# Expert gather, expert sum and out projection in the short float format; sum and norm tile by tile, recurrence roots ahead of the gates

## Chip, cores and metric

The kernel runs on 1 core of one Trainium2 chip. The metric is the device time of one execution in microseconds (us), the median of several runs; lower is better.

## What is computed

The reference runs two transformer blocks on 512 tokens of width 1024, all in float32. What matters here is the end of the first block and the mixing part of the second:

```python
# first block, end: hierarchical mixture of experts, 4 groups x 8 experts, top 2 in the best group
w_top, e_idx = lax.top_k(p_exp, TOP_K)                      # two experts for each token
w_top = w_top / jnp.sum(w_top, -1, keepdims=True) * p_group
for e in range(N_EXPERTS):                                  # 32 experts, 1024 -> 256 -> 1024
    hid = jax.nn.silu(t @ w_gate[e]) * (t @ w_up[e])
    out = out + combine[:, e:e + 1] * (hid @ w_down[e])
x = x + gate2[:, None, :] * ffn
# second block
f = swiglu(rms_norm_2(h, ffn1_norm_pre), w_gate, w_up, w_down)     # "ffn1", width 2816
h = h + 0.5 * rms_norm_2(f, ffn1_norm_post)
# mixing: dilated attention, and a linear recurrence  h_t = a_t h_(t-1) + b_t
b = jnp.sqrt(-jnp.expm1(2.0 * log_a)) * (gate_x * xc)
gates = jax.nn.sigmoid(gl)
merged = gates[:, :, 0] * attn_d + gates[:, :, 1] * rec_d
h = h + rms_norm_2(merged @ w_out, mix_norm_post)
f = swiglu(...)                                                    # "ffn2", then the last residual
```

## The kernel before

One program, written engine by engine: PE, ACT, DVE, POOL and SP each have a fixed list of instructions (bottom of the file), and they meet at counting semaphores (`nxt(engine, name)` waits for the next count). Activations lie transposed (features on partitions) in `hT`; the residual `X` lies by tokens, four tiles of 128.

**Two kinds of matmul.** A matmul on plain float32 operands leaves two records in the trace. In the ffn stages and most of the mixing the operands are split into a high part, rounded to the short format (`F32R`), and the rest: `three` (L2128) multiplies high*high, high*low and low*high, and each of these leaves one record. ACT makes the high part of each 1 MB weight slot (`act_high`, L2110), POOL the low part (L2115 and L2457, one subtraction of 128x2048), SP loads the next slot when `slots_used` says that PE has read the slot three places before (L2444).

**Router and gather (L1580 to L1756).** PE makes the logits (L1585) and turns the normed tokens back (`pe_h2`), ACT copies them to `h2tok` (`act_h2`, L1634) and only then computes the two exponentials of the router (`act_route`). DVE chooses the experts (L1663 to L1710); PE ranks the tokens (L1596 to L1602, L1598 counts tokens before, L1601 counts all); DVE gives each of the two choices of a token a place among 1024 (`r_place`, L1726). It then compares a row of numbers with the places, twice for each of 4 tiles (L1735), POOL adds each pair to the selection matrix `m_G` (L1756), and DVE makes the weighted matrix `m_C` (L1740, L1742). PE starts the gather (L1611, 64 float32 matmuls of 512 columns) when all four tiles of `m_G` are there, then turns `m_C` (L1619). `dve_more_list` lists the experts with more than 128 tokens; here there is one such item, which runs ahead of the others (`pe_more`).

**Experts (`pe_moe`).** Each of 32 experts reads 128 gathered places: gate and up (L1814), Silu on ACT, product on DVE (L1885), down (L1822), copied by ACT and DVE into `m_yT`.

**Sum (L2006 to L2044).** PE turns `m_yT` back to rows (L2015), ACT and DVE copy them, and PE sums with the weights of `m_CT` (L2023, 64 float32 matmuls). DVE adds the result times `gate2` to `X`. All engines meet, then `act_norm1`/`dve_norm1` norm the tiles, PE turns them (`pe_xT`, L2200), ACT and DVE split them (L2286, L2335), and ffn1 starts.

**Recurrence (L2954 to L2985).** For each of 8 blocks m DVE does a reciprocal (L2964), waits for the root from ACT (`act_roots`, L2924), does L2967, L2968, L2970, the scan (L2972) and, for m below 3, two attention products (L2951). On ACT `act_roots` stands between the first and the second slot of the gate `gl1`. At the end DVE multiplies by the Gelu (L2981), ACT takes the high parts (L2665), with `mix_high(REC_W + 2)` (the high part of a weight slot) behind the first of them, and DVE the low parts (L2984); then PE multiplies by `rec` (8 halves) and DVE merges each half (L2752 frees the bank, L2754 adds).

**Out projection (`pe_out2`, L2987).** 64 float32 matmuls of 512 columns on `merged` and raw weight slots; the last two slots are done tile by tile, and `act_between`/`dve_between` norm each tile as it comes.

## Time and profile before

| | us |
|---|---|
| median of 3 runs | 2647.72 (2644.58 to 2651.13) |
| the profiled execution | 2647.43 |
| its span, first to last instruction | 2645.6 |
| PE busy | 2415.2 (91%) |
| DVE, ACT, POOL busy | 863.8, 613.6, 597.4 |
| DMA | 277.97 MB, 105 GB/s in the mean |

The stages, by the profile's times from the start of the span: first block's attention and recurrence to 594, its out projection to 651, router and gather 667 to 795, experts 799 to 1164, sum and norm 1165 to 1249, ffn1 1249 to 1640, mixing 1645 to 2261, ffn2 2261 to the end. PE's busy time is modelled at each matmul's end, so the pace of matmuls is read from the distance of their starts.

### The profile page before, as it was taken

Reading aid. Unit: us, or ns where it says so; the run is one execution under the profiler, and the core shown is the slowest. Engines: PE = TensorE matmul, PEld = TensorE weight load, DVE = VectorE, ACT = ScalarE, POOL = GpSimd, SP = SyncE. Lnnn points to the kernel's source line nnn. Section 1 sums busy time; section 2 is a strip of 40 time slices with the busy share of each in tenths; the row PEclk is TensorE's granted clock in tenths of the full one; section 3 lists DMA queues with packets and bytes.
Section 4 is the critical chain, followed back from the end, with each engine's and each line's share of the span. In section 5 each row is a group of like instructions: output and inputs, shape, how many; then the busy total and the mean of one; then the engine's idle time right before and its main releaser. Section 6 shows DMA issues by size and latency. Waiting matters only on the chain.

```text
span 2645.6 us, 30301 instructions
## 1 busy us (share of the span) xinstructions
PE 2415.2 (91%) x12189; PEld 1873.7 (71%) x12190; DVE 863.8 (33%) x1288; ACT 613.6 (23%) x940; POOL 597.4 (23%) x216
## 2 busy tenths in 40 slices
PE   6998789958498999997999997999999979899998
PEld 5644468853448999984888786888875854688786
DVE  4275544431441111112222204143452952322302
ACT  2023223320201000012222214143323311322212
POOL 0023023300100000010344342333422420344432
PEclk7998879989599999998999998999999989899999
DMA  8221400001114888840322223212332221333222
GB/s 278 64 80 60 163 32 1 1 1 48 58 41 139 296 295 295 296 161 0 93 89 90 94 96 97 96 64 92 107 113 81 89 87 55 96 95 95 96 80 88
DMA packets 220357, 277.97 MB, mean 105 GB/s; under 512 B 9703, under 2 KB 199107, under 8 KB 220260
## 3 DMA queue, kind: packets, MB, share of 16 engines
q1 hardware_dynamic: 211744, 267.49, 30.6%
q10 hardware_dynamic: 7140, 4.87, 0.7%
q0 software_dynamic: 1376, 4.26, 0.5%
q8 instruction: 68, 1.11, 0.2%
q14 instruction: 29, 0.24, 0.0%
HBM read 272.36 MB, written 4.24 MB: 105 GB/s over the span
## 4 chain that ended last, share of the span: by engine, by line
PE 82%; DVE 8%; ACT 3%; issue 2%; DVEq 2%; ACTq 1%; DMA 1%; POOL 1%; POOLq 0%
PE bank L2131 39%; PE bank L1814 9%; PE bank L1822 4%; PE bank L618 3%; PE bank L1611 2%; PE bank L586 2%; PE bank L1504 2%; PE bank L2023 2%; PE bank L1294 1%; PE bank L434 1%; PE bank L2994 1%; DVE arena L2967 1%; PE bank L1287 1%; PE bank L2880 1%; PE bank L2899 1%
## 5 line engine op out<-in xcount | busy, mean ns | idle before, releaser
L2131 PE MATMUL bank<-hT_high_split,ring_split 128*128 128x512 f32 x2496 | 797.2, 399 | 8.1 <-DVEq L2232 5.6
L2131 PEld LDWEIGHTS bank<-hT_high_split,ring_split 128*128 128x128 f32 x2496 | 471.4, 189 | 120.0 <-DVEq L2232 6.3
L2115 POOL TENSOR_TENSOR ring_split<-ring,ring_split 128x2048 fp32r<-128x2048 f32 x66 | 304.4, 4614 | 1014.4 <-ACT ring_split L2110 1014.4
L2131 PE MATMUL bank<-hT_split,ring_split 128*128 128x512 f32 x1248 | 492.0, 394 | 0.0
L2110 ACT ACTIVATE ring_split<-ring 128x2048 fp32r<-128x2048 f32 x104 | 199.1, 1916 | 669.7 <-DMA ring<-in_ffn_w_up 197.4
L2131 PEld LDWEIGHTS bank<-hT_split,ring_split 128*128 128x128 f32 x1248 | 235.8, 189 | 57.2 <-issue 0.2
L2457 POOL TENSOR_TENSOR ring_split<-ring,ring_split 128x2048 fp32r<-128x2048 f32 x38 | 175.8, 4627 | 350.7 <-ACT ring_split L2110 350.7
L1814 PE MATMUL bank<-arena,ring 128*128 x2048 | 235.8, 276 | 5.5 <-issue 5.5
L1814 PEld LDWEIGHTS bank<-arena,ring 128*128 128x128 f32 x2048 | 233.1, 193 | 5.7 <-issue 5.7
L2131 PE MATMUL bank<-ring_split,hid_high_split 128*128 128x512 f32 x704 | 224.7, 401 | 8.1 <-DVE hid_low_split L2242 7.2
L2131 PEld LDWEIGHTS bank<-ring_split,hid_high_split 128*128 128x128 f32 x704 | 133.8, 191 | 42.2 <-DVE hid_low_split L2242 8.0
L2237 DVE TENSOR_TENSOR arena<-arena,bank 128x512 f32<-128x512 f32 x44 | 30.2, 687 | 348.4 <-ACT arena L2213 345.0
L2131 PE MATMUL bank<-ring_split,hid_low_split 128*128 128x512 f32 x352 | 140.8, 400 | 0.0
L1822 PE MATMUL bank<-arena,ring 128*128 128x128 f32 x1024 | 119.4, 275 | 0.0
L1822 PEld LDWEIGHTS bank<-arena,ring 128*128 128x128 f32 x1024 | 116.8, 192 | 0.0
L1885 DVE TENSOR_TENSOR arena<-arena,bank 128x256 f32<-128x256 f32 x32 | 13.5, 421 | 226.5 <-ACT arena L1864 226.5
L2240 DVE CAST hid_high_split<-arena 128x512 f32 (+1 forms) x44 | 80.7, 1833 | 7.0 <-issue 6.4
L618 PE MATMUL bank<-hT,ring 128*128 128x512 f32 x192 | 82.6, 592 | 0.0
L1350 POOL TENSOR_TENSOR arena<-arena,constants 128x512 f32<-128x512 f32 x40 | 50.8, 1286 | 128.5 <-PE bank L1287 79.6
L2131 PEld LDWEIGHTS bank<-ring_split,hid_low_split 128*128 128x128 f32 x352 | 67.0, 190 | 16.4
L1611 PE MATMUL bank<-arena 128*128 128x512 f32 x128 | 57.9, 616 | 22.3 <-POOL arena L1756 22.3
L2342 DVE TENSOR_SCALAR arena<-arena 128x1024 f32<-128x1024 f32 x2 | 5.3, 2652 | 202.5 <-DMA constants<-in_mix_norm_pre 102.0
(421 smaller groups left out, 2770.0 us busy)
## 6 DMA issues: line engine op xcount, KB each, us to landing
ring<-in_w_in SPq DMA_DIRECT2D x45, 1024.0 KB, 5.1
ring<-in_w_gate SPq DMA_DIRECT2D x32, 1024.0 KB, 5.5
ring<-in_w_up SPq DMA_DIRECT2D x32, 1024.0 KB, 8.0
ring<-in_w_down SPq DMA_DIRECT2D x32, 1024.0 KB, 7.5
ring<-in_ffn_w_gate SPq DMA_DIRECT2D x22, 1024.0 KB, 5.3
ring<-in_ffn_w_up SPq DMA_DIRECT2D x22, 1024.0 KB, 5.4
ring<-in_ffn_w_down SPq DMA_DIRECT2D x22, 1024.0 KB, 4.9
ring<-in_w_ada SPq DMA_DIRECT2D x16, 1024.0 KB, 5.2
```

Of the source, the lines that this page charges most:

```text
L586: mm = pe.matmul(banks[t][:, :], lhs(4 * half + k, t), w[:, k, :], start=(half == 0 and k == 0), stop=(half == 1 and k == 3))
L618: mm = pe.matmul(bank[j][:, :], w[:, k, j * P:(j + 1) * P], hT[:, k, :], start=(k == 0), stop=(k == KD - 1))
L1504: mm = pe.matmul(bank[2 * t + half][:, :], lhs(k, t), w[:, kk_, 512 * half:512 * half + 512], start=(k == 0), stop=(k == 2 * n_slots_ - 1))
L1611: mm = pe.matmul(bank[n % 8][:, :], h2tok[:, t, k * P:(k + 1) * P], m_G[:, t, 512 * half:512 * half + 512], start=(t == 0), stop=(t == NT ...
L1814: mm = pe.matmul(dst[:, c:c + CAP], w[:, u, k, f * P:(f + 1) * P], m_xT[:, k, bass.ds(at, CAP)], start=(k == 0), stop=(k == KD - 1))
L1822: mm = pe.matmul(dst[k // 4][:, (k % 4) * CAP:(k % 4 + 1) * CAP], w[:, f, k * P:(k + 1) * P], hid[:, f, :], start=(f == 0), stop=(f == 1))
L2023: mm = pe.matmul(bank[2 * t + half][:, :], m_CT[:, s, t * P:(t + 1) * P], m_y[:, s, 512 * half:512 * half + 512], start=(s == 0), stop=(s ...
L2110: act.activation(high(n), raw(n), ACT.Copy).then_inc(S(f"{tag}_high"), 1)
L2115: pool.tensor_tensor(low(n), raw(n), high(n).bitcast(F32), ALU.subtract)\
L2131: mm = pe.matmul(dst, left[l], right[r], start=start and n == 0, stop=stop and n == 2)
L2240: dve.tensor_copy(at[0], hid)
L2457: pool.tensor_tensor(low(n), raw(n), high(n).bitcast(F32), ALU.subtract).then_inc(S("mix_low"), 1)
```

## The change

- *Gather.* `m_G` is made on DVE alone (a comparison with a row of 1024 numbers, `iota_wide`, for the first choice, and a second one that adds), without POOL's addition, and a tile of it can be used as soon as it is there. It holds zeros and ones in the short format. The tokens are split into `h2_high` (ACT, beside `h2tok`) and `h2_low` (POOL, four subtractions of 128x1024), so the gather is two products of 64 short matmuls each. ACT does the group exponential ahead of the copies and the second one between them.
- *Ranks.* Five matmuls instead of fourteen.
- *Weights.* `m_C` is gone. PE makes `w_row` (the weight of each place, on all partitions) in 32 short matmuls, and DVE multiplies each expert's hidden values by it, one more 128x256 product for each expert. PE turns `m_G` instead of `m_C`.
- *Sum.* The turned rows are split into `y_high` (ACT) and `y_low` (DVE); the sum is 128 short matmuls, first the left half of the columns, then the right half tile by tile. Each tile goes into the norm at once; the meeting of the engines is gone. The high part of ffn1's second slot is made after the norm.
- *Recurrence.* `act_roots` stands ahead of the first slot of `gl1`.
- *Out projection.* The four weight slots of `w_out2` and `merged` are split, and `three` is used: 192 short matmuls.

```diff
@@ pe_route
-            nxt(pe, "h2_ready", NT)
+            nxt(pe, "h2_ready")
+            nxt(pe, "r_M")
+            pe.matmul(bank[2][:, 0:P], con("before"), r_M.rearrange("p t e -> p (t e)"), start=True, stop=False)
+            for t in range(NT - 1):
+                pe.matmul(bank[2][:, 32 * (t + 1):P], ones,
+                          r_M[:, t, :].unsqueeze(1).broadcast_to([P, NT - 1 - t, N_EXP]), start=False, stop=(t == NT - 2))
+            mm = pe.matmul(bank[2][:, P:2 * P], ones, r_M.rearrange("p t e -> p (t e)"), start=True, stop=True)
+            mm.then_inc(S("r_ranks"), 1)
+            nxt(pe, "h2_ready", NT - 1)
             pe.drain().then_inc(S("o_free"), 1)
...
+            for t in range(NT):
+                nxt(pe, "r_G")
+                for n in range(8):
+                    gather(n, h2_high, t, t == 0, False)
+            nxt(pe, "h2_low", NT)
+            for n in range(8):
+                for t in range(NT):
+                    mm = gather(n, h2_low, t, False, t == NT - 1)
+                mm.then_inc(S("m_x_ps"), 1)
+            for n in range(8, 2 * KD):
+                nxt(pe, ("m_x_even", "m_x_odd")[n % 2])
+                for part in (h2_high, h2_low):
...
+            nxt(pe, "w_split")
+            for half in range(2):
+                nxt(pe, ("m_x_even", "m_x_odd")[half])
+                terms = [(t, c, w) for t in range(NT) for c in range(2) for w in (r_wh, r_wl)]
...
@@ act_route
             act.drain().then_inc(S("r_gexp"), 1)
+            act_h2(act, 1)
+            act_h2(act, 2)
             nxt(act, "r_diff")
             act.activation(r_w2, r_m2, ACT.Exp).then_inc(S("r_wexp"), 1)
+            act_h2(act, 3)
+            act_h2(act, 0)
@@ dve_route
+            nxt(dve, "iota_wide")
+            for t in range(NT):
+                dve.tensor_scalar(m_G1[:, t, :], iota_wide, r_place[:, 0, t:t + 1], None, ALU.is_equal)
                 dve.drain()
+                dve.scalar_tensor_tensor(m_G[:, t, :], iota_wide, r_place[:, 1, t:t + 1], m_G1[:, t, :].bitcast(F32),
+                                         ALU.is_equal, ALU.add).then_inc(S("r_G"), 1)
@@ pool_route
+            for t in (1, 2, 3, 0):
+                nxt(pool, "h2_ready")
+                i = pool.tensor_tensor(h2_low[:, t, :], h2tok[:, t, :], h2_high[:, t, :].bitcast(F32), ALU.subtract)
+                i.then_inc(S("h2_low"), 1)
@@ dve_moe, hidden
+                dve.drain()
+                dve.tensor_tensor(m_hid[:, b], m_hid[:, b], weights_at(at), ALU.mult)
@@ pe_moe_end
             for s in range(8):
+                turn(0, s)
             nxt(pe, "gate_taken")
+            for s in range(8):
+                if s < 4:
+                    turn(1, s)
+                for t in range(NT):
+                    mm = add(bank[4 + t][:, :], 0, s, t)
+                if s >= 4:
+                    turn(1, s)
+            mm.then_inc(S("m_sum_ps"), 1)
+            nxt(pe, "y_low", 4)
+            for t in range(NT):
+                for s in range(8):
+                    mm = add(bank[t][:, :], 1, s, t)
                 mm.then_inc(S("m_sum_ps"), 1)
+                if t >= 2:
+                    pe_xT(pe, t - 2, FIRST_BANKS)
@@ dve_moe_end
+            nxt(dve, "m_sum_ps")
+            for t in range(NT):
+                total(t, 0)
+            nxt(dve, "post_loaded", 16)
             for t in range(NT):
                 nxt(dve, "m_sum_ps")
+                total(t, 1).then_inc(S("x_new"), 1)
+                if t:
+                    dve_unit(dve, t - 1)
+                if t >= 2:
+                    dve_xT(dve, t - 2, FIRST_BANKS)
@@ act_mix
+            act_roots(act)
             for n in range(GL1, YR):
-                if n == GL1 + 1:
-                    act_roots(act)
                 mix_high(act, n + 2)
...
+            for n in range(4):
+                if n < 3:
+                    mix_high(act, OUT2 + n)
+                nxt(act, "m_merged")
+                for m in (2 * n, 2 * n + 1):
+                    i = act.activation(merged_hi[m], merged[:, m, :], ACT.Copy)
+                i.then_inc(S("m_high"), 1)
+            mix_high(act, OUT2 + 3)
@@ dve_mix
                 dve.drain().then_inc(S("m_merged"), 1)
+                if n > REC_W:
+                    dve_merged(dve, n - REC_W - 1)
+            dve_merged(dve, 3)
+        def dve_merged(dve, n):
+            nxt(dve, "m_high")
+            for m in (2 * n, 2 * n + 1):
+                i = dve.tensor_tensor(merged_lo[:, m, :], merged[:, m, :], merged_hi[m].bitcast(F32), ALU.subtract)
+            i.then_inc(S("m_low"), 1)
@@ pe_out2, add
+                return three(pe, bank[2 * t + half][:, :], (merged_hi[k][:, c], merged_lo[:, k, c]),
+                             [x[:, kk_, r] for x in w], k == 0, k == KD - 1)
```

## Rows read from the trace of the kernel before

**Rows 1.** The page, part 4: the chain that ended last, by engine.
```profile
PE 82%; DVE 8%; ACT 3%; issue 2%; DVEq 2%; ACTq 1%; DMA 1%; POOL 1%; POOLq 0%
```
**Rows 2.** Windows: stretch, busy (x count) of PE, PEld, DVE, ACT, POOL, clock, DMA.
```profile
704.00:712.00 8.00, 6.05 (x28) 5.92 (x28) 1.54 (x8) 0.00 (x0) 0.00 (x0) 0.50 0.00 0
712.00:732.00 20.00, 0.00 (x0) 0.00 (x0) 19.16 (x18) 0.00 (x0) 10.12 (x4) 0.50 0.00 0
732.00:738.00 6.00, 5.68 (x7) 2.48 (x8) 5.74 (x6) 0.00 (x0) 0.26 (x1) 0.52 0.01 3
819.00:1164.00 345.00, 344.94 (x3071) 344.94 (x3072) 34.92 (x63) 30.87 (x63) 0.00 (x0) 0.99 0.81 274
1229.00:1250.00 21.00, 7.45 (x34) 6.35 (x35) 12.61 (x19) 13.33 (x23) 0.00 (x0) 0.67 0.00 0
2050.00:2126.00 76.00, 75.78 (x324) 60.37 (x322) 73.57 (x42) 26.59 (x29) 31.92 (x7) 1.00 0.28 91
```
**Rows 3.** The chain of waits in order of time: start, length, what.
```profile
732.32 57.91 PE bank L1611 x128
1173.31 55.19 PE bank L2023 x128
1249.26 237.26 PE bank L2131 x1008
2191.43 34.59 PE bank L2994 x80
```
**Rows 4.** Timeline, router and gather: start, length, engine, line, what.
```profile
701.09 0.22 ACT L1639 ACTIVATE arena<-arena 128x16 f32<-128x16 f32 x1
712.44 0.17 DVE L1729 TENSOR_SCALAR arena<-arena 128x8 f32<-128x8 f32 x1
725.26 2.34 POOL L1756 TENSOR_TENSOR arena<-arena 128x1024 f32<-128x1024 f32 x1 [2.33 <-DVEq L1737]
734.10 0.75 DVE L1740 TENSOR_SCALAR arena<-arena 128x1024 f32<-128x1024 f32 x1
734.94 1.28 DVE L1742 SCALAR_TENSOR_TENSOR arena<-arena 128x1024 f32<-128x1024 f32 x1
791.05 3.69 PE L1619 MATMUL bank<-constants,arena 128*128 128x128 f32 x32 [0.83 <-issue]
799.50 7.41 PE L1814 MATMUL bank<-arena,hT 128*128 x64 [0.37 <-issue]
```
**Rows 5.** Groups of DVE instructions by line and form: busy, mean ns.
```profile
L1735 DVE TENSOR_TENSOR arena<-constants,arena 128x1024 f32<-128x1024 f32 x8 | 15.9, 2033 | 0.4
L2697 DVE TENSOR_SCALAR arena<-arena 128x2 f32<-128x2 f32 x8 | 10.1, 1265 | 0.6
```
**Rows 6.** Timeline, end of the experts.
```profile
1165.30 7.18 PE L2015 MATMUL bank<-constants,arena 128*128 128x128 f32 x64 [1.01 <-DVEq L1893]
1166.40 0.69 DVE L2035 COPY arena<-bank 128x512 f32<-128x512 f32 x1 [1.27 <-PE bank L2015]
1233.72 0.29 ACT L2281 ACTIVATE rstd<-ss,constants 128x1 f32<-128x1 f32 x1
```
**Rows 7.** Timeline, recurrence.
```profile
2049.75 0.69 DVE L2967 SCALAR_TENSOR_TENSOR arena<-arena 128x512 f32<-128x512 f32 x1 [24.93 <-ACT arena L2924]
2088.09 4.65 POOL L2457 TENSOR_TENSOR ring_split<-ring,ring_split 128x2048 fp32r<-128x2048 f32 x1 [6.48 <-ACT ring_split L2110]
2088.37 4.91 DVE L2967 SCALAR_TENSOR_TENSOR arena<-arena 128x512 f32<-128x512 f32 x1
2133.03 4.83 POOL L2457 TENSOR_TENSOR ring_split<-ring,ring_split 128x2048 fp32r<-128x2048 f32 x1 [6.57 <-ACT ring_split L2110]
2138.94 4.89 DVE L2984 TENSOR_TENSOR hid_high_split<-arena,hid_low_split 128x512 fp32r<-128x512 f32 x8
2143.96 0.76 PE L2131 MATMUL bank<-hid_low_split,ring_split 128*128 128x512 f32 x1 [18.19 <-issue]
```
**Rows 8.** DMA issues between 2100 and 2200: KB each, median us to landing.
```profile
ring<-in_w_rec_branch SPq DMA_DIRECT2D x4, 1024.0 KB, 5.2
```

More of the change, by code:

```diff
@@ L3080, in _ @@
             act_high(act, "ffn1", 0)
-            act_high(act, "ffn1", 1)
-            meet(act)
             act_norm1(act)
@@ L3125, in _ @@
             pe_moe_end(pe)
-            meet(pe)
-            for t in range(NT):
-                pe_xT(pe, t)
+            for t in (2, 3):
+                pe_xT(pe, t, FIRST_BANKS)
             nxt(pe, "hT_low", NT)
```

255 lines of the change are left out of this document (135 added, 120 removed).

## The prediction

> **What bounds the kernel now.** I read the chain of waits first: 82% of it is PE [rows 1], so time goes where PE's own work shrinks or where PE stands still. The table of windows says which it is, stretch by stretch [rows 2]: the 32 experts (819 to 1164) are PE to the last microsecond, with DVE busy for 35 of 345 us; from 712 to 732 PE does nothing while DVE and POOL make the selection matrix; from 1229 to 1250 PE has 7.5 us of work while tiles are normed; from 2050 to 2126 PE is full again, and 18.19 us of standing still follow, until the first `rec` matmul at 2143.96 [rows 7]. The change touches the four places around these and leaves the experts and both ffn stages as they are.
>
> **The price of a matmul.** In the chain, float32 with 512 columns takes 57.91/128 = 0.452 us a record at the gather, 55.19/128 = 0.431 at the sum, 34.59/80 = 0.432 at the out projection [rows 3]; the calls number 64 each, so a call is two records, 0.865 us. A short one takes 237.26/1008 = 0.235 [rows 3]; I use 0.2325, the pace inside a half of 24 (5.58 us). So two products cost 0.465 and three 0.70 where float32 costs 0.865. PE alone: gather 57.9 to 29.8, sum 55.2 to 29.8, out projection 55.3 to 44.6, and 7.4 for the 32 matmuls of `w_row`. At the low clock (0.50 to 0.52 from 704 to 738 [rows 2]) a short matmul takes about 0.43, an estimate: half the rate.
> The Trainium skill (TensorE: Matmul & The Clock Gate, section "Wait — 56ns, not 53.3ns?") gives 215.7 ns between warm matmuls of 512 columns. The rows show 235; by that figure the 480 new matmuls would take some 8 us less. The sum goes by the rows.
>
> **Part 1, router to the first expert (PE's L1814, 799.50 [rows 4]).** Until the logits (692.7) nothing changes.
> *Ranks:* 28 records fill 6.05 us of PE [rows 2]; 10 records at that pace are 2.2, say 2.5: 3.6 earlier. *Exponential:* it ran at 701.09 [rows 4] behind four pairs of copies; now about 2 earlier. *Against it:* four subtractions of POOL at 2.34 [rows 4], started as ACT's copies come, between about 697 and 710. DVE and POOL get in each other's way: L1735 takes 2.03 us in the mean beside POOL [rows 5], against 1.28 for L1742, a longer operation of the same width [rows 4], and even a 128x2 operation takes 1.27 [rows 5] where a 128x8 one takes 0.17 [rows 4]. The tail of the router is a string of such small ones. With ACT's third copy waiting for DVE's `r_diff`, the subtractions pair up: two hold DVE to about 702, two more (705 to 710) hold the scan behind the ranks. I put `r_place` where it was, 712.3 (its first reader: 712.44 [rows 4]). Bounds: 6 earlier if nothing is held, 7 later if POOL gets in first each time.
> The Trainium skill (SBUF — State Buffer, section "Who interferes with whom") says that the loser waits for the whole instruction, as L1735 does, and that a DVE operation with at most one SBUF input, outside its two-port modes, never waits. No row here shows a reduction beside POOL; if these wait as well, the time is in B.
> *Selection matrix:* 0.75 + 1.28 + gaps [rows 4] = 2.1 a tile, four tiles by 720.7; PE starts at 714.5 instead of 732.32. The 32 matmuls on high parts end at 724.5 (the first dozen at the low clock), 32 on low parts 7.4, 64 more 14.9, `w_row` 7.4: 754.2. ACT and DVE empty the banks meanwhile; `dve_more_list` (9 us, now 722 to 731) ends just before DVE's first copy is wanted. Turning is the same 3.69 [rows 4], with DVE's two `w_row` copies: to 758.8. From the end of the turned copies to L1814 it was 4.1 (795.4 to 799.5): 762.9. **-36.5.**
> *Experts:* one product more on DVE for each, about 0.5. It lies beside 10.7 us of PE for each expert; only the one extra item, which runs alone, pays: **+0.6**.
>
> **Part 2, sum and norm (from L2015 at 1165.30 [rows 6] to ffn1's first matmul at 1249.26 [rows 3]: 83.96).** Counted from 1165.3. DVE now makes low parts at 0.69 [rows 6] plus gaps, so the left half is turned by 5 and summed by 23.6, the last low part is there at 25.1, and the right sums are ready at 28.8, 32.6 and 36.3. PE is not last any more; DVE is. ffn1's first weight slot is split at 26: POOL holds DVE's additions to 31, the four left results end at 34.5, the first right result at 35.9. Before, result, square, table load and root took 5.5 (sum's end at 1228.5 [rows 3], root's end at 1234.0 [rows 6]); with half a result it is 4.2, and tile 0 is normed at 40.5. Behind tile 2's sum PE has `pe_xT` of tile 0 and behind that tile 3's sum: PE waits from 36.3 to 40.5, turns, and sums tile 3 by 46 (warm) or 49 (cold). Then result, norm, turn, two splits: 56.7 to 59.9. I take 58: **-26**. Ends: -30 (POOL's subtraction doesn't hold DVE) and -20.
> The slot whose high part moved is wanted 11.2 us after the start of ffn1, and 2.0 + 4.7 are needed; ffn2 starts like that already.
>
> **Part 3, recurrence.** DVE's first L2967 waits 24.93 us for the root, at 2049.75 [rows 7]. Behind the slot's high part (ends 2036.2) the roots come at about 2038, 11.5 earlier. But DVE is then in step with POOL: L2967 takes 4.91 instead of 0.69 because POOL's subtraction started 0.28 before it [rows 7], and these come every 11.2 us at PE's pace. The last scan moves by one such round, 11.2, to 2118.5. Gelu 7 still needs PE's last matmul at 2125.8 (2143.96 - 18.19 [rows 7]). So L2981 ends at about 2128 instead of 2139, and then a queue decides: on ACT `mix_high(REC_W + 2)` stands between the first and the second high part of the recurrence. Its slot is asked for when PE has read the last `yr` slot, 2125.8, and lands 5.2 later [rows 8], at 2131.0, which is when it was used before. So POOL's subtraction stays at 2133.03 to 2137.86 [rows 7], DVE's low parts 1 to 7 (4.89/8 = 0.61 each [rows 7]) wait for it, and end at 2142.2 instead of 2143.8. **-1.7** where the move promises 11. Ends: 0 and -11.
>
> **Part 4, `rec` and out projection.** The new waits stand on DVE: `dve_merged(0)` and `(1)` wait for ACT's copies, which stand behind `mix_high` of a slot that was only just asked for (5.2 to land and 2.0 for ACT, which is 2133.03 - 2125.8 - 5.2), and then behind POOL's 4.7. Meanwhile L2752 can't free PE's banks. Slot OUT2 + 0 is asked for at 2166.5, DVE is free again at 2179.3, but bank 0 is wanted at 2177.7: 2.5 lost. The same at OUT2 + 1: DVE is free at 2190.6, the last bank at 2192.9. The out projection starts at 2193.0, against 2191.43 [rows 3]. Two slots take 22.4; slot OUT2 + 3 is split at 2216 (asked for at 2204.2, and some 11.8 as above): 0.5 lost. First tile at 2215.9 + 5.6 = 2221.5; before it was 2191.43 + 34.59 = 2226.0 [rows 3]. Behind it DVE's norm paces the tiles (7.2 each), not PE, so ffn2 starts as much earlier: -4.5, with part 3 in it. Of PE's 10.7 less only this is left. Ends: -1 and -16 with part 3.
>
> **Sum.** 2647.4 (profiled execution; the median of the runs is 0.3 more) - 36.5 + 0.6 - 26 - 4.5 = **2581**.
>
> **Rivals.** *A, the queues cost nothing:* DVE isn't held by POOL where I say so, and the moved roots carry through. For it: the windows in which they meet are a guess from start times. Against: L2967's eight rows. It gives 6 in part 1, 4 in part 2 and up to 12 in parts 3 and 4: 2559. Chance 0.17.
> *B, the new low-part chains are longer:* DVE behind POOL 7 later in part 1, the comparison at 1.28 instead of 0.75 (+2), tile 3 summed cold and six late in part 2, nothing kept in parts 3 and 4 (+4.5): 2600. Chance 0.17.
> *C, slower than before:* the clock stays low for the new matmuls. They come in stretches between waits; from 1229 to 1250 the clock is 0.67, after 712 it is 0.50 [rows 2]. At 0.43 each the 480 cost 96 us more: 2677. It decides from 330 of the 480 (66/0.2). Against: from 2050 to 2126 short matmuls run at 1.00, and float32 ones got it back within 6 us of 732. Chance 0.02.
> *D, it doesn't do what it says:* three quarters of the gather's gain needs the tile-by-tile start; if all waits for `h2_low` come first (POOL late beyond 724), PE stands: some 8 less of gain, 2589, inside my range. Chance 0.04 by itself. My forecast within 10 us: 0.60.
>
> **Chances and range.** Range 2557 to 2603: it reaches A's and B's times. 0.3% (8 us) is about what a measurement of this kernel can tell from no change. Faster by more: 0.96; within: 0.01; slower: 0.03.
>
> **What would show it.** Gather: about 128 + 32 short records at 0.233, first at 714 to 715, the first expert item at 763. If `r_place` is nearer 706, POOL held nothing. Sum: DVE, not PE, on the chain from 1165 + 25 on, and a gap of PE before `pe_xT` of tile 0. Recurrence: DVE's wait before the first L2967 gone, but PE's gap before `rec` 16 to 17 us instead of 18.2, with POOL's L2457 in front of L2984. Out projection: two short gaps of PE in `rec`, caused by L2752. The prediction is wrong if PE's records for the short form are slower than 0.24, if an expert takes more than 10.7 us of PE, or if PE's gap before `rec` shrinks to under 10.

## The result, and the profile after

The changed kernel takes 2582.36 us (median of 4 runs, 2579.50 to 2585.58), the kernel before 2646.66 us on the same chip: ratio 0.9755, 95% interval 0.9735 to 0.9775. On a second chip it was 2581.0 us and 0.9746 (0.9732 to 0.9760). The forecast was 2581. The profiled execution has a span of 2577.7 us and a granted clock of 0.948, as before.

| stretch, from profiled executions | before, us | after, us | shift | forecast |
|---|---|---|---|---|
| start to logits (DVE's L1666, after L1708) | 692.70 | 689.72 | -3.0 | 0 |
| logits to the first item of an expert (L1814, L1864) | 106.80 | 69.06 | -37.7 | -36.5 |
| first item to the first turned tile | 365.80 | 366.43 | +0.6 | +0.6 |
| first turned tile (start of L2015, L2070) to ffn1's first matmul | 83.96 | 55.96 | -28.0 | -26 |
| ffn1 to PE's last stretch of projections ahead of `rec` (`gl1` and `yr`; 2035.38, 1968.76) | 786.12 | 787.59 | +1.5 | 0 |
| from there to ffn2's first matmul | 226.22 | 223.25 | -3.0 | -4.5 |
| ffn2 to the end | 384.0 | 385.7 | +1.7 | 0 |
| sum | | | -67.9 | -66.4 |

So two places carry it, the gather and the sum with its norm, as forecast; recurrence and out projection together give 3 us.

The page's chain of the end, by engine (before: [rows 1]):
```profile
PE 84%; DVE 6%; ACT 3%; issue 2%; DMA 2%; DVEq 1%; ACTq 1%; POOL 1%; POOLq 0%
```
PE's share went up and DVE's down by the same two points. Added up by stretch, what DVE lost on the chain is the recurrence: from the last projections ahead of `rec` to ffn2 the chain held 89 us of DVE before and holds 23 now. In the router (660 to 800) DVE's part rose from 14 to 20 us, in the sum and norm from 8 to 15.

The gather in the chain of waits (start, length, what; before: [rows 3], [rows 4]), and windows of it (stretch, busy and count of PE, PEld, DVE, ACT, POOL, clock, DMA; before: [rows 2]):
```profile
710.44 31.78 PE bank L1621 x128
742.22 7.39 PE bank L1644 x32
749.62 3.51 PE bank L1655 x32
```
```profile
704.00:712.00 8.00, 2.02 (x6) 1.43 (x6) 6.88 (x12) 0.00 (x0) 2.33 (x2) 0.50 0.00 1
710.00:720.00 10.00, 9.56 (x32) 7.63 (x33) 9.40 (x24) 0.00 (x0) 0.00 (x0) 0.75 0.01 2
720.00:742.00 22.00, 22.00 (x97) 17.99 (x96) 9.47 (x15) 4.78 (x8) 0.00 (x0) 1.00 0.30 96
```
128 short matmuls stand where 128 records of 0.452 us stood. The first 32 take 9.6 us, because they begin at the low clock (0.75 in the mean of that window); the other 96 run at 0.23 each and PE never waits. The stretch is 26.1 us shorter (31.78 against 57.91 us) and starts 21.9 us sooner (710.44 against 732.32); `w_row` takes 7.4 of that back.

The router's small operations beside POOL (timeline: start, length, engine, line, what):
```profile
693.64 4.66 POOL L1802 TENSOR_TENSOR h_low_moe<-arena,low_end_moe 128x1024 fp32r<-128x1024 f32 x2 [27.81 <-ACTq L1672]
693.78 2.28 DVE L1727 SCALAR_TENSOR_TENSOR arena<-arena 128x32 f32<-128x32 f32 x1
696.13 0.19 DVE L1729 TENSOR_REDUCE arena<-arena 128x4 f32<-128x32 f32 x1
696.39 1.96 DVE L1696 TENSOR_TENSOR arena<-arena 128x32 f32<-128x32 f32 x1
701.67 4.65 POOL L1802 TENSOR_TENSOR h_low_moe<-arena,low_end_moe 128x1024 fp32r<-128x1024 f32 x2 [3.37 <-ACTq L1672]
704.50 0.29 DVE L1755 TENSOR_REDUCE arena<-bank 128x32 f32<-128x128 f32 x1 [2.69 <-PE bank L1614]
704.86 1.54 DVE L1757 TENSOR_TENSOR_SCAN arena<-arena 128x32 f32<-128x32 f32 x1
```
POOL's four subtractions of 2.33 us come in two pairs, as the prediction had it. Three of DVE's operations of 128x32, which take 0.19 to 0.23 us otherwise, last until a subtraction ends: 2.28, 1.96, 1.54. The scan behind the ranks is one of them. Two reductions did not wait: the one at 704.50, whose input is a PSUM bank, took 0.29, and the one at 696.13, whose single input is in SBUF, took 0.19 beside POOL's second subtraction (695.97 to 698.31). The prediction had left open whether reductions wait; these do not.

The sum and the norm:
```profile
1150.66 4.68 POOL L2204 TENSOR_TENSOR ring_split<-ring,ring_split 128x2048 fp32r<-128x2048 f32 x1 [444.34 <-ACT ring_split L2199]
1151.56 4.34 DVE L2110 TENSOR_TENSOR residual<-residual,arena 128x512 f32<-128x512 f32 x1
1155.82 0.68 DVE L2108 TENSOR_TENSOR arena<-bank,arena 128x512 f32<-128x512 f32 x1
1164.44 1.09 PE L2291 MATMUL bank<-constants,arena 128*128 128x128 f32 x8 [3.46 <-DVE arena L2419]
1181.17 0.79 PE L2220 MATMUL bank<-hT_high_split,ring_split 128*128 128x512 f32 x1 [2.79 <-DVEq L2322]
```
DVE's second addition of the left half takes 4.34 us instead of 0.69: it stands behind POOL's subtraction of ffn1's first slot (1150.66 to 1155.34). PE waits 3.46 us before it turns tile 0.

The recurrence (before: [rows 7]):
```profile
1971.48 3.27 DVE L3068 SCALAR_TENSOR_TENSOR arena<-arena 128x512 f32<-128x512 f32 x1 [13.28 <-ACT arena L3025]
2051.55 9.32 DVE L3082 TENSOR_TENSOR arena<-arena 128x512 f32<-128x512 f32 x8
2059.43 0.62 ACT L2746 ACTIVATE hid_low_split<-arena 128x512 fp32r<-128x512 f32 x1
2064.12 1.91 ACT L2199 ACTIVATE ring_split<-ring 128x2048 fp32r<-128x2048 f32 x1 [4.07 <-DMA ring<-in_w_rec_branch]
2066.11 4.52 POOL L2539 TENSOR_TENSOR ring_split<-ring,ring_split 128x2048 fp32r<-128x2048 f32 x1 [6.38 <-ACT ring_split L2199]
2066.58 8.20 DVE L3085 TENSOR_TENSOR hid_high_split<-arena,hid_low_split 128x512 fp32r<-128x512 f32 x7 [5.10 <-ACT hid_low_split L2746]
2074.91 0.76 PE L2220 MATMUL bank<-hid_low_split,ring_split 128*128 128x512 f32 x1 [16.02 <-issue]
```
DVE's wait before its first L3068 fell from 24.93 to 13.28 us. But ACT makes one of its eight copies (2059.43), then waits 4.07 us for a weight slot to land, and only behind that slot's high part come the other seven. POOL's subtraction of the slot then stretches DVE's seven low parts to 8.20 us. PE's gap is 16.0 where it was 18.2.

The chain of waits shows the same turn. In the kernel before it ran through DVE's scans from 2049.75 to the product at 2129.80; in the changed kernel it runs through PE up to its last matmul ahead of `rec`, and then through the transfer. First the piece before, then the two after:
```profile
2129.80 0.70 DVE arena L2981
```
```profile
1969.32 89.59 PE bank L2220 x384
2058.93 5.17 DMA ring<-in_w_rec_branch
```

The out projection:
```profile
2107.94 4.76 DVE L2852 TENSOR_TENSOR hid_high_split<-arena,hid_low_split 128x512 fp32r<-128x512 f32 x2 [6.46 <-ACT hid_low_split L2755]
2113.44 0.47 PE L2220 MATMUL bank<-hid_low_split,ring_split 128*128 128x512 f32 x1 [2.27 <-DVE arena L2841]
2119.01 4.80 DVE L2852 TENSOR_TENSOR hid_high_split<-arena,hid_low_split 128x512 fp32r<-128x512 f32 x2 [3.55 <-ACT hid_low_split L2755]
2127.25 0.70 PE L2220 MATMUL bank<-ring_split,hid_low_split 128*128 128x512 f32 x2 [0.82 <-issue]
```
DVE stands 6.46 us for ACT's copies and then works 4.76 instead of 1.29 beside POOL; PE waits 2.27 us for a bank. The 0.82 us at 2127.25 stand ahead of the first matmul of the out projection, where the kernel before has 0.83.

### The profile page after: what moved, and what is told of

Read it like the earlier page. It is cut to its first block, busy times and chain, and to the rows that moved or that the text cites. A ratio compares the mean times of both kernels' runs of the same rounds, so it can differ in the third digit from the quotient of the medians.

```text
span 2577.7 us, 30715 instructions
## 1 busy us (share of the span) xinstructions
PE 2364.3 (92%) x12267; PEld 1889.2 (73%) x12268; DVE 895.6 (35%) x1332; ACT 633.0 (25%) x968; POOL 620.4 (24%) x228
## 4 chain that ended last, share of the span: by engine, by line
PE 84%; DVE 6%; ACT 3%; issue 2%; DMA 2%; DVEq 1%; ACTq 1%; POOL 1%; POOLq 0%
PE bank L2220 43%; PE bank L1864 9%; PE bank L1872 5%; PE bank L626 3%; PE bank L594 2%; PE bank L1512 2%; PE bank L1302 2%; PE bank L442 1%; PE bank L1621 1%; PE bank L2981 1%; PE bank L1295 1%; PE bank L3000 1%; DMA ring<-in_ffn_w_down 1%; PE bank L614 1%; PE bank L910 1%
## 5 line engine op out<-in xcount | busy, mean ns | idle before, releaser
L2204 POOL TENSOR_TENSOR ring_split<-ring,ring_split 128x2048 fp32r<-128x2048 f32 x66 | 305.3, 4627 | 920.7 <-ACT ring_split L2199 920.7
L2199 ACT ACTIVATE ring_split<-ring 128x2048 fp32r<-128x2048 f32 x108 | 206.9, 1916 | 710.4 <-DMA ring<-in_ffn_w_up 196.2
L2539 POOL TENSOR_TENSOR ring_split<-ring,ring_split 128x2048 fp32r<-128x2048 f32 x42 | 194.8, 4640 | 382.9 <-ACT ring_split L2199 382.9
L2220 PE MATMUL bank<-ring_split,hid_high_split 128*128 128x512 f32 x784 | 251.2, 398 | 7.8 <-DVE hid_low_split L2332 7.1
L1864 PE MATMUL bank<-arena,ring 128*128 x2048 | 235.9, 276 | 5.3 <-issue 5.3
L1864 PEld LDWEIGHTS bank<-arena,ring 128*128 128x128 f32 x2048 | 233.2, 193 | 5.4 <-issue 5.4
L2220 PEld LDWEIGHTS bank<-ring_split,hid_high_split 128*128 128x128 f32 x784 | 148.1, 189 | 45.2 <-DVE hid_low_split L2332 8.0
L2220 PE MATMUL bank<-ring_split,hid_low_split 128*128 128x512 f32 x464 | 175.7, 398 | 1.4 <-issue 0.8
L2220 PEld LDWEIGHTS bank<-ring_split,hid_low_split 128*128 128x128 f32 x464 | 87.3, 189 | 23.4 <-issue 1.2
L626 PEld LDWEIGHTS bank<-hT,ring 128*128 128x128 f32 x192 | 36.5, 190 | 45.5 <-issue 45.4
```

Source lines behind the costliest of these rows:

```text
L626: mm = pe.matmul(bank[j][:, :], w[:, k, j * P:(j + 1) * P], hT[:, k, :], start=(k == 0), stop=(k == KD - 1))
L1864: mm = pe.matmul(dst[:, c:c + CAP], w[:, u, k, f * P:(f + 1) * P], m_xT[:, k, bass.ds(at, CAP)], start=(k == 0), stop=(k == KD - 1))
L2199: act.activation(high(n), raw(n), ACT.Copy).then_inc(S(f"{tag}_high"), 1)
L2204: pool.tensor_tensor(low(n), raw(n), high(n).bitcast(F32), ALU.subtract)\
L2220: mm = pe.matmul(dst, left[l], right[r], start=start and n == 0, stop=stop and n == 2)
L2539: pool.tensor_tensor(low(n), raw(n), high(n).bitcast(F32), ALU.subtract).then_inc(S("mix_low"), 1)
```

## The experiments

The total is a blunt measure here. In the profiled executions of these kernels, the code ahead of the logits, which is the same in all of them, ended anywhere between 686 and 696 us. Distances inside one stage agree better: from the first turned tile to ffn1 it is 55.95 to 56.03 us in the eleven profiles of kernels in which that stage is as in the changed kernel. So each verdict below rests on a distance of its own stage, with the total beside it. S1 is from the start of `pe_h2`'s turns to the end of the gather (changed kernel: 52.7; 52.2 to 52.7 in the eleven profiles with that stage unchanged), S2 from the first turned tile to ffn1 (56.0), G is PE's gap before `rec` (16.0), S3 from the first matmul of the last projections ahead of `rec` (1968.76 in the changed kernel) to ffn2 (221.9 to 223.6 in the five profiles with that stage unchanged).

| kernel | median us | ratio to before (95%) | S1 | S2 | G | S3 |
|---|---|---|---|---|---|---|
| before | 2646.7 | 1 | | 84.0 | 18.2 | 226.2 |
| changed | 2582.4 | 0.9755 (0.9735-0.9775) | 52.7 | 56.0 | 16.0 | 223.2 |
| changed, again | 2581.0 | 0.9746 (0.9732-0.9760) | 52.7 | 56.0 | 16.0 | 221.9 |
| roots_back | 2588.5 | 0.9769 (0.9750-0.9788) | 52.2 | 56.0 | 18.1 | 230.6 |
| roots_exact | 2582.9 | 0.9751 (0.9735-0.9768) | 52.4 | 56.0 | 18.1 | 224.1 |
| high_last | 2571.4 | 0.9704 (0.9685-0.9724) | 52.4 | 56.0 | 6.9 | 214.0 |
| roots_back_high_last | 2582.5 | 0.9745 (0.9724-0.9766) | 52.2 | 56.0 | 13.7 | 226.7 |
| roots_exact_high_last | 2580.6 | 0.9737 (0.9715-0.9758) | 52.4 | 56.0 | 13.7 | 220.1 |
| copies_first | 2579.3 | 0.9728 (0.9710-0.9747) | 52.4 | 56.0 | 15.9 | 219.5 |
| out_f32 | 2581.5 | 0.9752 (0.9736-0.9768) | 52.6 | 56.0 | 16.0 | 224.7 |
| slot0_early | 2575.7 | 0.9728 (0.9712-0.9745) | 52.4 | 50.8 | 16.2 | 223.3 |
| waits_all | 2585.9 | 0.9763 (0.9748-0.9778) | 58.9 | 56.0 | 16.0 | 222.9 |
| no_low | 2571.5 | 0.9716 (0.9698-0.9733) | 46.2 | 56.0 | 16.3 | 223.6 |
| three_edits | 2558.4 | 0.9665 (0.9647-0.9683) | 52.4 | 50.8 | 6.9 | 209.7 |

**Does a queue eat the moved roots?** The theory says that the gain of 11 us is hidden behind one weight slot in ACT's queue. It is tried from both ends: put the roots back, take the slot out of the way, and do both.

```
# roots_back, in act_mix
-            act_roots(act)
             for n in range(GL1, YR):
                 mix_high(act, n + 2)
+                if n == GL1 + 1:
+                    act_roots(act)
```


> The changed kernel with the recurrence's square roots back where they were, behind the second `gl1` slot of ACT's queue. My theory: the move of the roots is eaten by ACT's and POOL's queue ahead of `rec` (the high part of slot REC_W + 2 stands between the recurrence's copies and lands no earlier), so undoing it costs 2 to 3 us: PE's gap before `rec` 16.0 -> 18 to 19 us, total about 2585. The rival, that the moved roots carry through and what is seen as the gap has another origin: undoing it costs the whole 11 us by which DVE's first multiplication of the recurrence now starts earlier, gap 27, total about 2593.

Measured: G is 18.1, as the theory said, but S3 is 7.3 to 8.7 us longer than in the two profiles of the changed kernel. A second gap of PE, 3.48 us at 1995.23, stands 26 us into the stretch, which the kernel before does not have: PE waits there for ACT to empty a bank, and ACT is busy from 1987.60 with the eight roots and the two table loads around them (6.9 us). The edit was not what the expectation called it: before, the roots stood ahead of the second slot's high part, here behind it. So it priced another order, and the comparison was made again with the exact one.

```
# roots_exact, in act_mix
-            act_roots(act)
             for n in range(GL1, YR):
+                if n == GL1 + 1:
+                    act_roots(act)
                 mix_high(act, n + 2)
```


> The changed kernel with the roots exactly where the kernel before had them: ahead of the high part of ACT's second `gl1` slot, not behind it. The run with them behind it had a new gap of PE of 3.5 us at that slot, which the kernel before hasn't, and so doesn't price the move. My theory: PE's gap before `rec` returns to the 18.2 us of the kernel before (16.0 in the changed kernel) and no other gap appears: 2 to 3 us slower than the changed kernel, the first `gl1` matmul to the first of `rec` 108 us instead of 105.6. The rival: that other run's 7.4 us on this stretch were the price of the move itself, then 113 us here too.

The timeline of roots_exact:
```profile
1988.40 0.69 DVE L3069 SCALAR_TENSOR_TENSOR arena<-arena 128x512 f32<-128x512 f32 x1 [24.92 <-ACT arena L3026]
2068.13 9.22 DVE L3083 TENSOR_TENSOR arena<-arena 128x512 f32<-128x512 f32 x8
2082.29 0.76 PE L2220 MATMUL bank<-hid_low_split,ring_split 128*128 128x512 f32 x1 [18.10 <-issue]
```
The wait of the kernel before is back (24.93 in [rows 7]), the gap too (18.10 against 18.19), and no other gap appears. DVE's eight products start 94.1 us behind the first matmul of the stretch here and 82.8 behind it in the changed kernel: the move brings them 11.3 us forward, one round of weights, and PE sees 2.1 of it. The chains before and after say why: with the roots late the end hangs on DVE, with the roots early on PE's last matmul and on the slot asked for then. The rival (113 us for the stretch) is out; it was 108.

```
# high_last, in act_mix
             for m in range(KD):
                 nxt(act, "l_rec")
                 act.activation(rec_hi[:, m, :], l_r(m), ACT.Copy).then_inc(S("rec_high"), 1)
-                if m == 0:
-                    mix_high(act, REC_W + 2)
+            mix_high(act, REC_W + 2)
             mix_high(act, REC_W + 3)
```


> The changed kernel with the high part of weight slot REC_W + 2 moved behind all eight copies `rec_hi` of ACT, instead of behind the first. My theory, the queue: ACT's copies run from 2059.4 on without a break and end at about 2064, DVE's low parts follow 0.6 us behind each and end before POOL begins on the slot, so PE's gap before `rec` falls from 16.0 to about 7 us; total -9, about 2573. The rival, that DVE's own scans are what `rec` waits for: the gap stays at 16 (0 us), since the last product of the recurrence comes no earlier. A middle case, POOL's subtraction of the slot before still holds DVE: -4 to -5.

The timeline of high_last:
```profile
2061.47 4.25 ACT L2746 ACTIVATE hid_low_split<-arena 128x512 fp32r<-128x512 f32 x8
2062.86 4.90 DVE L3084 TENSOR_TENSOR hid_high_split<-arena,hid_low_split 128x512 fp32r<-128x512 f32 x8
2066.12 1.91 ACT L2199 ACTIVATE ring_split<-ring 128x2048 fp32r<-128x2048 f32 x1 [0.40 <-DMA ring<-in_w_rec_branch]
2067.88 0.76 PE L2220 MATMUL bank<-hid_low_split,ring_split 128*128 128x512 f32 x1 [6.95 <-issue]
2068.11 4.54 POOL L2539 TENSOR_TENSOR ring_split<-ring,ring_split 128x2048 fp32r<-128x2048 f32 x1 [6.33 <-ACT ring_split L2199]
```
Eight copies in one piece, eight low parts in 4.90 us, PE at work 0.23 us before POOL starts on the slot: gap 6.9. The slot lands just then (ACT waits 0.40 us for it), so it loses nothing by its new place; in the changed kernel it was seven copies that waited for it. One line moved in a queue gives four times what the moved roots give.

The roots late in that kernel, first in the wrong order and then in the exact one:

> Both edits: roots behind the second `gl1` slot again, and slot REC_W + 2 split behind all of ACT's copies. If the queue is what eats the gain of the moved roots, then without that queue the place of the roots counts in full: this kernel is 8 to 11 us slower than the one with the slot's high part last alone, and about as fast as the changed kernel itself or 2 us slower (gap before `rec` 16 to 18 us, total 2582 to 2584). If the roots' place never mattered (PE's last matmul of `yr` and Gelu 7 set the end either way), this one equals the kernel with the high part last: about 2573.

> The same, and slot REC_W + 2 split behind all of ACT's copies. With the high part last alone the gap before `rec` is 6.9 us. If the queue hid the move's worth, then here, with the queue gone and the roots late, DVE's chain of scans sets the end: gap 13 to 15 us (last scan, eight products and eight low parts of 0.61 us each), the stretch 103 to 104 us, 6 to 8 us slower than with the high part last alone. If the roots' place is worth as little as in the changed kernel (2.4 us), gap about 9.

The first has a gap of 13.7 before `rec`, where 16 to 18 was expected, and the extra gap (3.54 us) in front. Its total of 2582.5 lies in the expected 2582 to 2584, but by two gaps where the theory had one; its price too is that of the other order. The second, in its timeline:
```profile
2069.25 4.84 ACT L2747 ACTIVATE hid_low_split<-arena 128x512 fp32r<-128x512 f32 x8 [1.42 <-DVE arena L3082]
2073.35 4.90 DVE L3085 TENSOR_TENSOR hid_high_split<-arena,hid_low_split 128x512 fp32r<-128x512 f32 x8
2075.97 6.68 POOL L2539 TENSOR_TENSOR ring_split<-ring,ring_split 128x2048 fp32r<-128x2048 f32 x1 [10.18 <-ACT ring_split L2199]
2078.38 0.77 PE L2220 MATMUL bank<-hid_low_split,ring_split 128*128 128x512 f32 x1 [13.70 <-issue]
```
Gap 13.7, inside the 13 to 15 expected. The four gaps make the interplay: with the slot in the queue the roots' place is worth 2.1 us (18.1 to 16.0), without it 6.8 (13.7 to 6.9). The rest of the 11 stays hidden even then, since Gelu 7 needs PE's last matmul. Here it was POOL that lost: 6.68 us instead of 4.6 beside DVE's low parts.

**What does splitting the out projection give?**

```
# out_f32: the out projection of the kernel before
-                return three(pe, bank[2 * t + half][:, :], (merged_hi[k][:, c], merged_lo[:, k, c]),
-                             [x[:, kk_, r] for x in w], k == 0, k == KD - 1)
+                return pe.matmul(bank[2 * t + half][:, :], merged[:, k, c], w[:, kk_, r],
+                                 start=(k == 0), stop=(k == KD - 1))
...
-        SPLIT = [n for n in range(N_MIX) if not LRU <= n < GL1]
+        SPLIT = [n for n in range(OUT2) if not LRU <= n < GL1]
```
ACT's copies of `merged` and DVE's low parts of it are left out with it.

> The changed kernel with the out projection as before: float32 matmuls on the whole `merged` and whole weight slots, nothing split for it by ACT, POOL or DVE; all else as changed. By PE's work alone it costs 10.7 us. My theory: waits have taken the place of this work (2.27 + 0.82 us inside `rec`, the first slot split 5 us after PE could start, the last slots 12 us after they are asked for), so from the first `rec` matmul to the first of ffn2 it takes 117 to 120 us against 117.1 in the changed kernel and 117.6 in the kernel before; total +0.5 to +3, about 2584. The rival, PE's saving counts somewhere behind: +8 to +11, about 2592.

Measured: from the first `rec` matmul to ffn2's first 118.6 us, against 117.1 and 115.7 in the two profiles of the changed kernel; ratio 0.9752, between the changed kernel's two. So a part of the change with some 10.7 us less work for PE (an estimate from the prices of a matmul) is worth 1.5 to 2.9 us. Inside `rec` PE does not wait here, where the changed kernel waits 2.27; the 0.83 us ahead of the out projection are there too.

```
# copies_first, in act_mix
             for n in range(4):
-                if n < 3:
-                    mix_high(act, OUT2 + n)
                 nxt(act, "m_merged")
                 for m in (2 * n, 2 * n + 1):
                     i = act.activation(merged_hi[m], merged[:, m, :], ACT.Copy)
                 i.then_inc(S("m_high"), 1)
-            mix_high(act, OUT2 + 3)
+                mix_high(act, OUT2 + n)
```


> The changed kernel with ACT taking the copies of `merged` for pair n ahead of the high part of slot OUT2 + n, not behind it. My theory: PE's short gaps inside `rec` (2.27 and 0.82 us) and the late start of the out projection come from DVE standing at its low parts of `merged` behind ACT's wait for a slot that has not landed; the gaps go, the out projection starts 4 to 5 us earlier counted from the first `rec` matmul (52.3 -> 48), the first tile is done 5 us earlier; total about -5, 2577. The rival: the lag is of DMA and POOL (slot OUT2 + 0 is wanted as soon as it is split), so the start of the out projection moves by under 1 us.

DVE's low parts of `merged` and a window of PE in copies_first, then the window behind the gap in the two profiles of the changed kernel, in which the gap is 2.27 and 2.33 us (columns as above):
```profile
2105.08 1.29 DVE L2850 TENSOR_TENSOR hid_high_split<-arena,hid_low_split 128x512 fp32r<-128x512 f32 x2
2116.28 1.29 DVE L2850 TENSOR_TENSOR hid_high_split<-arena,hid_low_split 128x512 fp32r<-128x512 f32 x2
2090.00:2125.00 35.00, 35.00 (x152) 28.24 (x151) 10.87 (x16) 8.86 (x9) 12.62 (x3) 1.00 0.26 90
```
```profile
2113.00:2120.00 7.00, 6.56 (x22) 5.22 (x23) 3.26 (x5) 2.95 (x3) 1.98 (x1) 0.76 0.35 142
```
```profile
2113.00:2120.00 7.00, 6.73 (x29) 5.50 (x30) 3.32 (x5) 2.95 (x3) 2.22 (x1) 1.00 0.33 133
```
The low parts take 1.29 us and no longer 4.76, and the 2.27 us gap is gone; the one of 0.82 stays (the expectation had both gone; it belongs to the start of the out projection). From the first `rec` matmul to the out projection it is 48.6 us instead of 52.3 and 51.0 in the two profiles of the changed kernel, to the first finished tile 77.7 instead of 81.4 and 80.0, and S3 is 2.4 to 3.8 us shorter. Against the second profile the saving is 2.4, the gap itself. Against the first it is 3.7, because there the granted clock fell behind the gap: 0.76 over 7 us, and the 48 matmuls up to the out projection took 13.0 us; in the second it stayed at 1.00, and they took 11.4. So the theory holds, at 2.4 to 3.7 where it said 4 to 5.

**What holds the sum?**

```
# slot0_early, in act_moe_end
                     act.activation(y_high[:, s, 512 * half:512 * half + 512], bank[s % 4][:, :], ACT.Copy)\
                        .then_inc(S("y_high"), 1)
+                    if half == 1 and s == 3:
+                        act_high(act, "ffn1", 0)
...
             act_moe_end(act)
-            act_high(act, "ffn1", 0)
```


> The changed kernel with the high part of ffn1's first weight slot taken inside ACT's loop of `act_moe_end`, behind the fourth copy of the right half, where ACT waits for turned tiles. My theory: POOL's subtraction then runs at about 1140 to 1144.5, beside low parts that read PSUM, and no longer at 1150.7 where it holds DVE's first addition (4.34 us instead of 0.69); the sum's first results come 3.6 us earlier, PE's wait of 3.46 us for the first normed tile shrinks and the last tile's sum doesn't start at the low clock (2 us). From the first turned tile to ffn1's first matmul 56.0 -> 51 to 52; total -4 to -5, about 2578. The rival, DVE's own chain of four results and norms sets the pace wherever POOL stands: under 1 us. A third: POOL now holds the low parts of the turned tiles, 0 to +4.

The timeline of slot0_early:
```profile
1143.02 4.60 POOL L2206 TENSOR_TENSOR ring_split<-ring,ring_split 128x2048 fp32r<-128x2048 f32 x1 [432.97 <-ACT ring_split L2201]
1145.27 0.69 DVE L2118 TENSOR_TENSOR ring_split<-bank,expert_out_moe 128x512 fp32r<-128x512 f32 x1 [3.40 <-ACT expert_out_moe L2102]
1154.85 0.69 DVE L2112 TENSOR_TENSOR residual<-residual,arena 128x512 f32<-128x512 f32 x1
1164.14 1.04 PE L2293 MATMUL bank<-constants,arena 128*128 128x128 f32 x8
1179.32 0.79 PE L2222 MATMUL bank<-hT_high_split,ring_split 128*128 128x512 f32 x1 [2.82 <-DVEq L2324]
```
POOL's 4.60 us lie beside a DVE operation with one PSUM input, which takes its 0.69; the addition that took 4.34 takes 0.69; PE turns tile 0 without a wait, and S2 is 50.8 instead of 56.0, in this kernel and again in three_edits. The theory's -4 to -5 was -5.1. Of it 3.6 us is the turn of tile 0, which comes 35.6 us behind the first turn instead of 39.2; the rest is tile 3's sum, whose 16 matmuls took 5.4 us in the changed kernel, the first eight at 0.43 each behind PE's wait, while the granted clock here is 1.00 from 1164 to 1171.
What these lines show agrees with the Trainium skill (SBUF — State Buffer, section "Who interferes with whom"): a DVE instruction with at most one SBUF input, outside its two-port modes, does not contend with GpSimd, one with two does if GpSimd reads SBUF, and whoever issues first keeps the shared port for its whole instruction. POOL's 6.68 us above go beyond one instruction: it started at 2075.97, took 2.1 us more than 4.6, and DVE's row of low parts ended at 2078.25, so POOL stood behind several of them in a row.

**What bounds the gather?**

```
# waits_all, in pe_route
+            nxt(pe, "r_G", NT)
             for t in range(NT):
-                nxt(pe, "r_G")
                 for n in range(8):
                     gather(n, h2_high, t, t == 0, False)
```


> The changed kernel, but PE waits for all four tiles of the selection matrix before its first gather matmul, instead of tile by tile. My theory: the last tile is ready at 716.4 us, 6.0 after PE's first matmul now (710.44); 32 matmuls take 7.4 us at full clock and 3 more if the first dozen run at the low one, so the high parts end at 724 to 727 instead of 720.0, and everything behind shifts by that, since PE is never short of a free bank there: +4.4 to +7, total about 2588. The rival, DVE's list of routed rows (ends 725.7) and its bank copies set the pace behind, so the tile-by-tile start buys under 1 us.

In its timeline PE's first matmul comes behind a wait of 12.07 us, not 6.0:
```profile
723.03 9.82 PE L1621 MATMUL bank<-places_moe,low_end_moe 128*128 128x512 f32 x32 [12.07 <-DVE places_moe L1774]
```
S1 is 6.2 us longer than in the two profiles of the changed kernel, the total 4.9 against the changed kernel on the same chip. The 32 matmuls take 9.82 us here without a wait between them, 0.31 each, and 9.6 tile by tile at a clock of 0.75: the waits between tiles cost next to nothing. So the tile-by-tile start is worth its 6 us in full.

```
# no_low, in pe_route (h2_low's product is left out; its wait stands ahead, where it costs nothing)
+            nxt(pe, "h2_low", NT)
             for t in range(NT):
                 nxt(pe, "r_G")
                 for n in range(8):
-                    gather(n, h2_high, t, t == 0, False)
-            nxt(pe, "h2_low", NT)
-            for n in range(8):
-                for t in range(NT):
-                    mm = gather(n, h2_low, t, False, t == NT - 1)
-                mm.then_inc(S("m_x_ps"), 1)
+                    mm = gather(n, h2_high, t, t == 0, t == NT - 1)
+                    if t == NT - 1:
+                        mm.then_inc(S("m_x_ps"), 1)
...
-                for part in (h2_high, h2_low):
-                    for t in range(NT):
-                        mm = gather(n, part, t, part is h2_high and t == 0, part is h2_low and t == NT - 1)
+                for t in range(NT):
+                    mm = gather(n, h2_high, t, t == 0, t == NT - 1)
```


> Left out: the product of the gather with the low part of the token rows (the experts' inputs are then only the high parts of the chosen rows). The subtractions of POOL stay. By PE's time the 64 matmuls cost 14.8 us. My theory: the first 32 hide something, namely DVE's list (up to 725.7 us), behind which stands its copy of bank 1; without them PE stands from 723 until 726.5, then one product of each bank follows at 0.93 us: x^T done at about 733 to 734 instead of 742.1, total -8 to -9, about 2574. The rival, PE alone bounds this stretch: -14.8, about 2568.

A row and two windows of no_low:
```profile
723.30 9.16 PE L1621 MATMUL bank<-places_moe,low_end_moe 128*128 128x512 f32 x28 [5.49 <-DVE arena L1782]
717.00:723.00 6.00, 0.81 (x4) 0.33 (x2) 5.12 (x9) 0.95 (x2) 0.00 (x0) 0.89 0.00 0
723.00:733.00 10.00, 9.70 (x32) 7.70 (x33) 4.61 (x8) 1.79 (x3) 0.00 (x0) 0.72 0.65 211
```
With 14.8 us of PE's work gone, S1 is 6.5 us shorter than in the changed kernel (52.7 against 46.2; total 9.5 on the same chip). PE stands 5.49 us for DVE's first copy of a bank (L1782, behind DVE's list), and the 28 matmuls behind that gap take 9.16 us, 0.33 each, at a clock of 0.72. The theory had the gap and not the clock behind it (-8 to -9 forecast). PE alone as the bound is refuted: 32 of the 64 low products are what DVE's list lies beside.

**The three moves together.** high_last, copies_first and slot0_early in one kernel:

> The changed kernel with the three moves of ACT's queue together: slot REC_W + 2's high part behind all copies of the recurrence, the copies of `merged` ahead of the high parts of OUT2, and ffn1's first slot taken inside the copies of the experts' sum. If they lie one behind the other and no saving is given back, the stages add: 9.1 + 3.7 + 5.1 = 17.9 us, 2564 to 2565, ratio to the kernel before 0.969. If POOL's subtractions, now at other times, hold DVE somewhere new, up to 5 of it are lost: 2570.

> The changed kernel as it is, on the same chip as the three runs beside it, as their yardstick: 2582 us within 3. One earlier comparison on another chip put it at 0.9755 of the kernel before; the run with all three moves should be 17 to 18 us below it here.

```profile
2059.89 0.76 PE L2222 MATMUL bank<-hid_low_split,ring_split 128*128 128x512 f32 x1 [6.94 <-issue]
```
G 6.9, S2 50.8, S3 12.2 to 13.6 shorter: the stages add to 17.4 to 18.8 us, where 17.9 was expected, and the two profiled spans differ by 18.7 (2556.5 and 2575.2). The medians differ by 22.6 (2558.4, where 2564 to 2565 was expected), some 4 more than the stages show; the runs of one kernel spread by up to 10 us, so I put no cause to that. At 0.9665 (0.9647 to 0.9683) of the kernel before it is the fastest of all, and from the changed kernel it differs by nothing but the order of ACT's queue.

Not run, each by itself: the five-matmul ranks, the moved exponentials, `w_row` with DVE's extra product, and the norm tile by tile. Their shares of the gather's and the sum's gain are argued from rows, not shown.

## Why the prediction was right, step by step

The mechanism was right in all four places, and the sizes of the two large parts within 2 us. That the total came out within 2 us is luck in part: -3.0 ahead of the logits, where nothing was changed, -1.2 and -2.0 in parts 1 and 2 lie against +1.5 in part 4 and +1.5 and +1.7 in stages that were left as they are.

**Price of a matmul.** 0.2325 forecast, 0.23 measured from 720 to 742. The main term stood on that, and it could be read from ffn1's rows before anything was changed. The Trainium skill (TensorE: Matmul & The Clock Gate, section "Wait — 56ns, not 53.3ns?") gives 215.7 ns for back-to-back matmuls of 512 columns on a warm array; no stretch here shows it, the closest being these 0.23. The prediction's estimate of 8 us by that figure goes with 0.2325; with the 0.235 that stands beside it there, it would be 9.

**Part 1** (-36.5, measured -37.7). The order of events came as told: two pairs of POOL's subtractions, the scan held, `r_place` 18.5 us behind the logits (forecast 19.6), PE's first matmul 2.3 us behind it, w_row's end 39.2 us behind the start (forecast 39.7), first item at 758.8 (forecast 762.9). Of these 4.1 us, 3.0 lie ahead of the logits, where nothing was changed and executions differ by up to 10 us. waits_all gives the share of the tile-by-tile start: 6.2.

**Part 2** (-26, measured -28.0). The named hold-up was there: POOL holds DVE's additions until 1155.3, 30.1 us behind the first turn (forecast 31); the left results end at 33.4 (34.5), PE turns tile 0 at 39.2 (40.5), tile 3 is summed at 45.4 (46 or 49), ffn1 starts at 56.0 (58). Each step is a little early, and the sum is inside its ends of -20 and -30. The end of -30 was said to be the price without POOL's hold-up; slot0_early is that case and gave -33: the term was 5.1 us, not 4, and 1.6 of it is the clock behind PE's wait.

**Part 3** (-1.7, measured -2.2 in the gap). The prediction's sharpest claim: a move that brings DVE's chain 11 us forward moves PE by under 2, because of `mix_high(REC_W + 2)` between the copies. roots_exact shows 11.3 and 2.1, high_last shows that the slot is the cause. One sign did not come: DVE's wait before the first L2967 was to be gone, and 13.28 us of it stayed. The prediction's own text had the roots 11.5 us earlier (measured: 11.7), which leaves about that much of the 24.93.

**Part 4** (-4.5 with part 3, measured -3.0, and -4.3 in the second profile of the changed kernel). Mechanism right, and the size differs from profile to profile. PE waits 2.27 us at L2841 (forecast 2.5) and 0.61 at 2150.49, for slot OUT2 + 3 (forecast 0.5). The sign said two short gaps inside `rec`; there is one, since the 0.82 ahead of the out projection is no new wait. From the first `rec` matmul to the first finished tile 79.2 us were forecast, and 81.4 and 80.0 measured. The term that was missing is the clock behind a wait: PE's 48 matmuls behind the 2.27 us take 13.00 us, 0.27 each instead of 0.2325. The prediction counted the wait at its length; in the first profile it cost 1.8 us more, in the second, with 11.4 us for the 48, next to nothing more.

**What hardly counted.** The stages left as they are moved by +1.5 and +1.7 us. Rival A (no queue costs) is refuted by the holds of 2 to 5 us in the rows above, B (longer chains) by the 69.06 us of part 1 and by S2, C (clock stays low for the short matmuls) by 1.00 from 720 on. D's mechanism, PE waiting for `h2_low`, did not occur: POOL was done at 706.3, before PE's first matmul. Its share was wrong as well: the tile-by-tile start is worth 6.2 of 37.7 us (waits_all), about a sixth and not three quarters of the gather's gain.

## What to carry to other kernels

A transfer's wait in an engine's in-order queue is as much a part of the critical path as the computing: ask of each instruction that waits for a DMA what stands behind it, and move it behind everything that can already run. A saving of matmuls counts only where PE is last; 14.8 us less work gave 6.5 in the gather and 10.7 less gave 1.5 to 2.9 in the out projection. To undo a part for a test, copy the old order exactly: one place off in a queue cost a new gap of 3.5 us and read like the price of the part.

## What the hardware showed that was not expected

- A gap of PE can cost more than its length, but does not always. Ten profiles have the wait of 2.02 to 2.33 us inside `rec` (2113.44 in the changed kernel). In nine the granted clock over the next 7 us was 0.76, and the 48 matmuls behind it took 13.0 us instead of the 11.2 that 0.2325 each makes; in one, of the same changed kernel, it was 1.00, and they took 11.4. A wait of 2.18 us that all fourteen profiles have (1912.43 in the changed kernel) was followed by 0.76 in six of them and by 1.00 in eight. Behind 5.49 us (723.30 in no_low) it was 0.72 over 10 us, and 28 matmuls took 9.2 us instead of 6.5. The two profiles of the changed kernel differ in S3 (223.2 and 221.9) by little else.
- Small DVE operations with two SBUF inputs are held like large ones, until POOL's instruction ends: 128x32 took 2.28 and 1.96 us beside a POOL subtraction of 2.33, a scan of 128x32 took 1.54 instead of 0.23. Those with one of two inputs, or their only one, in a PSUM bank were not held (0.69 and 0.29), and neither was a reduction with its single input in SBUF (0.19).
- The first quarter of the program, identical in all kernels, ended between 686 and 696 us from one profiled execution to another; a stage of 56 us in the middle repeated within 0.08. Differences of a few us are seen in stage distances, not in totals.
